# Attention's 128-row scores in a fused two-block kernel: three products of split operands in place of one f32 product

## The reference, cut to what matters

```python
q = (rms_norm(q_lat, q_norm) @ w_q_up).reshape(B, S, 16, 128 + 64)
kv = (rms_norm(kv_lat, kv_norm) @ w_kv_up).reshape(B, S, 16, 128 + 128)
q_nope, k_nope, v = q[..., :128], kv[..., :128], kv[..., 128:]
# q_rope, k_rope: the 64 rotary rows, k_rope shared by the heads
s = (einsum('bqhd,bkhd->bhqk', q_nope, k_nope)
     + einsum('bqhr,bkr->bhqk', q_rope, k_rope)) * ATTN_SCALE
p = softmax(where(causal, s, -1e30))          # in blocks of 128 queries
o = einsum('bhqk,bkhd->bqhd', p, v)
out = (o.reshape(B, S, 2048) * silu(z)) @ w_out
```

## Time and profile before

| what | us |
|---|---|
| median of three runs | 2210.17 |
| lowest and highest | 2209.99 and 2212.29 |
| the profiled execution's own time | 2210.97 |
| span of its trace | 2209.2 |
| TensorE busy (PE) | 2172.9, 98% |
| VectorE (DVE), ScalarE (ACT), GpSimd (POOL) busy | 1074.0, 939.5, 1068.4 |

### The profile page before, as it was taken

One profiled execution on the slowest core, in us unless ns is written; L12 is line 12 of the kernel. 1 busy time (PEld: TensorE's weight loads), 2 busy tenths in 40 slices (PEclk: granted clock), 3 DMA queues, 4 the chain that ended last, 5 costly groups with the idle time before them and its releaser, 6 DMA issues.

```text
span 2209.2 us, 33303 instructions
## 1 busy us (share of the span) xinstructions
PE 2172.9 (98%) x10972; PEld 1772.6 (80%) x10972; DVE 1074.0 (49%) x1498; ACT 939.5 (43%) x1638; POOL 1068.4 (48%) x787
## 2 busy tenths in 40 slices
PE   8999999999999999999999999999999999999999
PEld 6888888888888888788778878888778777888886
DVE  7842224444442262666524832236666638666512
ACT  4343333444433343555433244334454645444422
POOL 5654445445454444444355654444431634555553
PEclk9999999999999999999999999999999999999999
DMA  4332323233322333211132233333220022233333
GB/s 141 95 105 95 95 86 105 95 97 100 97 95 95 100 95 95 68 58 59 38 98 94 89 102 96 100 99 98 89 74 22 1 75 69 95 95 96 99 106 108
DMA packets 53791, 194.33 MB, mean 88 GB/s; under 512 B 6096, under 2 KB 6352, under 8 KB 53712
## 3 DMA queue, kind: packets, MB, share of 16 engines
q1 hardware_dynamic: 52704, 191.13, 27.5%
q10 hardware_dynamic: 1008, 2.14, 0.3%
HBM read 191.14 MB, written 2.10 MB: 87 GB/s over the span
## 4 chain that ended last, share of the span: by engine, by line
PE 73%; issue 15%; POOL 9%; DVE 1%; ACT 1%; POOLq 0%; DVEq 0%; ACTq 0%
PE proj L692 19%; PE proj L693 19%; PE proj L694 19%; POOL w_lo L621 9%; PE aux L850 2%; PE proj L875 1%; PE proj L803 1%; PE proj L805 1%; PE proj L804 1%; PE aux L861 1%; PE proj L973 1%; PE aux L973 1%; PE proj L1261 1%; PE proj L1262 1%; PE proj L1263 1%
## 5 line engine op out<-in xcount | busy, mean ns | idle before, releaser
L621 POOL TENSOR_TENSOR w_lo<-w_stage,w_hi 128x512 fp32r<-128x512 f32 x716 | 989.8, 1389 | 995.2 <-ACT w_hi L1323 995.0
L1323 ACT ACTIVATE w_hi<-w_stage 128x512 fp32r<-128x512 f32 x716 | 442.4, 628 | 805.3 <-PE proj L694 741.3
L692 PE MATMUL proj<-xh,w_hi 128*128 128x512 f32 x1696 | 666.3, 393 | 1.2 <-POOL w_lo L621 1.2
L694 PE MATMUL proj<-xh,w_lo 128*128 128x512 f32 x1696 | 660.1, 389 | 0.0
L693 PE MATMUL proj<-xl,w_hi 128*128 128x512 f32 x1696 | 660.1, 389 | 0.0
L692 PEld LDWEIGHTS proj<-xh,w_hi 128*128 128x128 f32 x1696 | 318.4, 188 | 74.6 <-POOL w_lo L621 5.6
L693 PEld LDWEIGHTS proj<-xl,w_hi 128*128 128x128 f32 x1696 | 318.4, 188 | 67.7 <-issue 2.4
L694 PEld LDWEIGHTS proj<-xh,w_lo 128*128 128x128 f32 x1696 | 318.4, 188 | 66.4
L692 PE MATMUL proj<-act_h,w_hi 128*128 128x512 f32 (+1 forms) x840 | 327.1, 389 | 2.8 <-POOL w_lo L621 2.8
L694 PE MATMUL proj<-act_h,w_lo 128*128 128x512 f32 (+1 forms) x840 | 326.8, 389 | 0.0
L693 PE MATMUL proj<-act_l,w_hi 128*128 128x512 f32 (+1 forms) x840 | 326.8, 389 | 0.0
(11 more groups left out here) (344 smaller groups left out, 2345.5 us busy)
## 6 DMA issues: line engine op xcount, KB each, us to landing
w_stage<-stream SPq DMA_DIRECT2D x358, 512.0 KB, 3.5
out<-x_res SPq DMA_DIRECT2D x3, 512.0 KB, 2.6
x_res<-x SPq DMA_DIRECT2D x2, 512.0 KB, 8.2
consts_sb<-consts ACTq DMA_DIRECT2D x1, 640.0 KB, 4.0
x_res<-x ACTq DMA_DIRECT2D x1, 512.0 KB, 7.5
out<-x_res SPq DMA_DIRECT2D x2, 256.0 KB, 2.2
x_res<-x SPq DMA_DIRECT2D x1, 256.0 KB, 3.5
x_res<-x ACTq DMA_DIRECT2D x1, 256.0 KB, 5.0
```

What stands on the lines that cost most here:

```text
L621: pool.tensor_tensor(w_lo[:, at, :], w_stage[:, at, :], w_hi[:, at, :].bitcast(F32), ALU.subtract).then_inc(stage_free, 1)
L692: pe.matmul(o, w_hi[:, slot, cols], hi, start=(b == 0), stop=False)
L694: mm = pe.matmul(o, w_lo[:, slot, cols], hi, start=False, stop=(b == blocks - 1))
L1323: act.activation(w_hi[:, u % RING, :], w_stage[:, u % RING, :], ACT.Copy).then_inc(hi_done, 1)
```

## The change

- The operands `qn` and `kn` (f32) are replaced by high and low parts in fp32r: `q_even` and `q_odd` for pairs of even and odd number, and `k_parts`, which is kept once and not twice. `qr` is kept once as well. Two placeholders move where tiles lie in SBUF.
- ScalarE now copies each q and k tile from its up-projection bank (`q_hi`, `k_hi`); VectorE waits for that (`q_high`, `k_high`) and subtracts the high part from the same bank; the bank is free after the subtraction.
- TensorE makes three fp32r products for each head and row block.
- ScalarE's list: q_hi(p+1, 0) comes after heads_hi(p-1) and before copy_turned(p, 0); q_hi(p+1, 1) after the w_hi that follows it; k_hi(0) after copy_turned(p, 2), then rope_hi(p+1), k_hi(1) and only then the w_hi that stood before rope_hi. In front of the loop q_hi twice, three w_hi, k_hi(0), rope_hi(0), k_hi(1), one w_hi.
- VectorE's and TensorE's lists keep their order; GpSimd and SyncE are not touched.

```diff
--- before.py
+++ after.py
@@ -350,15 +352,20 @@
...
-        qn = sb("qn", [P, 2, 2, S], F32, over)
-        kn = sb("kn", [P, 2, 2, S], F32, over)
-        qr = sb("qr", [P, 2, S], F32, over)
+        q_even = sb("q_even", [P, 2, 2, S], F32R, over)
+        k_parts = sb("k_parts", [P, 2, 2, S], F32R, over)
+        qr = sb("qr", [P, S], F32, over)
...
@@ -455,6 +462,7 @@
         k_rot_done = sem("k_rot_done")
         k_rope_hi, k_rope_lo = sem("k_rope_hi"), sem("k_rope_lo")
         q_rope_hi, q_rope_lo = sem("q_rope_hi"), sem("q_rope_lo")
+        q_high, k_high = sem("q_high"), sem("k_high")
         ready = sem("ready")
         dve_step = sem("dve_step")
         consts2_loaded = sem("consts2_loaded")
@@ -541,6 +549,11 @@
         def two_norms(n):
 
             return phases[n + 1] == "mixer"
+
+        HIGH, LOW = range(2)
+
+        def q_part(p, h, part):
+            return q_odd[2 * part + h][:, :] if p % 2 else q_even[:, part, h, :]
 
         def up_bank(j):
             return proj[:, 2 + j % 2, :]
@@ -847,7 +860,10 @@
                         pe.wait_ge(pt_done, n - 1)
                     q = slice(qb * P, w)
                     for h in range(2):
-                        pe.matmul(score_banks(qb, w)[:, h, :], qn[:, p % 2, h, q], kn[:, p % 2, h, 0:w], start=True, stop=False)
+                        o, q_h, q_l = score_banks(qb, w)[:, h, :], q_part(p, h, HIGH), q_part(p, h, LOW)
+                        pe.matmul(o, q_h[:, q], k_parts[:, HIGH, h, 0:w], start=True, stop=False)
+                        pe.matmul(o, q_h[:, q], k_parts[:, LOW, h, 0:w], start=False, stop=False)
+                        pe.matmul(o, q_l[:, q], k_parts[:, HIGH, h, 0:w], start=False, stop=False)
                     for h in range(2):
                         pe.matmul(score_banks(qb, w)[:, h, :], q_rope[:, h, q], k_rope_h[:, 0:w], start=False, stop=False)
                         mm = pe.matmul(score_banks(qb, w)[:, h, :], q_rope[:, h, q], k_rope_l[:, 0:w], start=False, stop=True)
@@ -1447,6 +1463,18 @@
                         act.activation(k_rope_h[:, :], k_rot[:, :], ACT.Copy).then_inc(k_rope_hi, 1)
                 assert unit.n == attention_unit + 4
                 v_tiles = iter([j for j, (kind, _, _) in enumerate(UP_TILES) if kind == "v"])
+                q_tiles = iter([j for j, (kind, _, _) in enumerate(UP_TILES) if kind in ("q0", "q1")])
+                k_tiles = iter([j for j, (kind, _, _) in enumerate(UP_TILES) if kind in ("k0", "k1")])
+
+                def q_hi(p, h):
+                    j = next(q_tiles)
+                    up_ready(act, j, attention_unit)
+                    act.activation(q_part(p, h, HIGH), up_bank(j), ACT.Copy).then_inc(q_high, 1)
+
+                def k_hi(h):
+                    j = next(k_tiles)
+                    up_ready(act, j, attention_unit)
+                    act.activation(k_parts[:, HIGH, h, :], up_bank(j), ACT.Copy).then_inc(k_high, 1)
 
                 def take_v(quad, blk):
                     j = next(v_tiles)
@@ -1475,15 +1503,20 @@
                     act.wait_ge(up_taken, 6 * p + 5)
                     for h in range(2):
                         half = slice(64 * h, 64 * h + 64)
-                        act.activation(q_rope[half, h, :], qr[half, p % 2, :], ACT.Copy).then_inc(q_rope_hi, 1)
+                        act.activation(q_rope[half, h, :], qr[half, :], ACT.Copy).then_inc(q_rope_hi, 1)
 
                 def heads_hi(p):
                     for h in range(2):
                         act.wait_ge(og_done, 2 * p + h + 1)
                         act.activation(act_h[:, 2 * p + h, :], og[:, h, :], ACT.Copy).then_inc(ah_done, 1)
 
-                his(4)
+                q_hi(0, 0)
+                q_hi(0, 1)
+                his(3)
+                k_hi(0)
                 rope_hi(0)
+                k_hi(1)
+                his(1)
                 for blk in range(4):
                     take_v(0, blk)
                 his(2)
@@ -1495,9 +1528,12 @@
                         his(1)
                     if p:
                         heads_hi(p - 1)
+                    if more:
+                        q_hi(p + 1, 0)
                     copy_turned(p, 0)
                     if more:
                         his(1)
+                        q_hi(p + 1, 1)
                     copy_turned(p, 1)
                     expo(p, 2)
                     if more:
@@ -1505,8 +1541,10 @@
                     expo(p, 3)
                     copy_turned(p, 2)
                     if more:
+                        k_hi(0)
+                        rope_hi(p + 1)
+                        k_hi(1)
                         his(1)
-                        rope_hi(p + 1)
                     copy_turned(p, 3)
                     if p < HEAD_PAIRS - 2:
                         take_v(p // 2 + 1, 2 * (p % 2))
@@ -2006,26 +2044,30 @@
                     return up_bank(j)
 
                 def take_q(p, h):
-                    took(dve.tensor_copy(qn[:, p % 2, h, :], next_up()))
+                    b = next_up()
+                    dve.wait_ge(q_high, 2 * p + h + 1)
+                    took(dve.tensor_tensor(q_part(p, h, LOW), b, q_part(p, h, HIGH).bitcast(F32), ALU.subtract))
 
                 def take_rope(p):
                     b = next_up()
                     link(dve.tensor_tensor(q_sin[:, :], b, sn[:, :], ALU.mult))
-                    took(dve.tensor_tensor(qr[:, p % 2, :], b, cs[:, :], ALU.mult))
+                    took(dve.tensor_tensor(qr[:, :], b, cs[:, :], ALU.mult))
 
                 def take_swap(p):
-                    took(dve.tensor_tensor(qr[:, p % 2, :], qr[:, p % 2, :], next_up(), ALU.add))
+                    took(dve.tensor_tensor(qr[:, :], qr[:, :], next_up(), ALU.add))
 
                 def rope_lo(p):
 
                     dve.wait_ge(q_rope_hi, 2 * p + 2)
                     for h in range(2):
                         mine, other = slice(64 * h, 64 * h + 64), slice(64 - 64 * h, 128 - 64 * h)
-                        dve.tensor_tensor(q_rope[other, h, :], qr[mine, p % 2, :], q_rope[mine, h, :].bitcast(F32),
+                        dve.tensor_tensor(q_rope[other, h, :], qr[mine, :], q_rope[mine, h, :].bitcast(F32),
                                           ALU.subtract).then_inc(q_rope_lo, 1)
 
                 def take_k(p, h):
-                    took(dve.tensor_copy(kn[:, p % 2, h, :], next_up()))
+                    b = next_up()
+                    dve.wait_ge(k_high, 2 * p + h + 1)
+                    took(dve.tensor_tensor(k_parts[:, LOW, h, :], b, k_parts[:, HIGH, h, :].bitcast(F32), ALU.subtract))
 
                 def row_max(p, qb):
```

More of the change, by code:

```diff
@@ L306, in program @@
         k_rope_l = sb("k_rope_l", [P, S], F32R, stat_over)
+        sb("sums_and_cosines", [P, 2, S], F32, stat_over)
+        q_odd = [sb("q_odd0", [P, S], F32R, stat_over)]
         stat_over.close()
@@ L352, in program @@
         lat_h = sb("lat_h", [P, 5, S], F32R, over)
-        k_rot = sb("k_rot", [P, S], F32, over)
+        turned_over = ExitStack()
+        k_rot = sb("k_rot", [P, S], F32, turned_over)
+        turned_over.close()
+        q_odd.append(sb("q_odd1", [P, S], F32R, over))
         zs = sb("zs", [P, IT, S], F32, over)
@@ L356, in program @@
         q_sin = sb("q_sin", [P, S], F32, over)
-        qn = sb("qn", [P, 2, 2, S], F32, over)
-        kn = sb("kn", [P, 2, 2, S], F32, over)
-        qr = sb("qr", [P, 2, S], F32, over)
+        q_even = sb("q_even", [P, 2, 2, S], F32R, over)
+        k_parts = sb("k_parts", [P, 2, 2, S], F32R, over)
+        qr = sb("qr", [P, S], F32, over)
+        q_odd.append(sb("q_odd2", [P, S], F32R, over))
         sn = sb("sn", [P, S], F32, over)
         og = sb("og", [P, 2, S], F32, over)
+        q_odd.append(sb("q_odd3", [P, S], F32R, over))
         over.close()
```

## The result

The changed kernel took 2228.81 us (median of four, 2227.76 to 2229.42) where the kernel before took 2211.23 on the same chip (2209.99 to 2212.31): **slower by 0.79%**, ratio 1.0079 with a 95% interval of 1.0067 to 1.0090. The profiled execution took 2227.76 us with a span of 2226.0, 16.8 longer than the span before. The forecast was +11.0 us, so the direction and the two stalls were right and the size was not: 2228.81 lies 1.8 us outside the range.

The account below looks back on a forecast made before the run. TensorE, 98% busy at full clock, was taken as the bound, with other engines deciding at two waits. Terms -5.2 + 12.2 + 3.0 + 0.7 + 0.3 = +11.0 us gave a median of 2221.2 us, range 2214.5 to 2227.

Parts of the forecast that it names:

- the two stalls: TensorE waits longer for k0's bank, 1.74 us in seven turns, and for ScalarE's turned copy, 0.5 us in six pairs.
- products: Attention scores: three fp32r products replace each f32 product, gaining 0.65 us per pair, 5.2 us for eight pairs.
- k banks, seven: k1 waits for ScalarE's copy and VectorE's subtraction of k0: 1.74 us later in seven turns, 12.2 us.
- q banks, six: q_hi(p+1, 0) ahead of copy_turned(p, 0) delays row block 2's scores 0.5 us in pairs 1 to 6: 3.0 us.
- start: In pair 0, k1 and v1 wait for ScalarE's copies of k, so the scores begin 0.7 us later.
- moved his(1): ScalarE's w_hi copy, moved behind k_hi(1), is used some 7 us later, so the delay costs nothing.
- last turn beside its k and products: Without v tiles, k1's load to the next scores takes 5.4 us instead of 5.1, for rope_lo: +0.3 us.
- an engine busy 43%: ScalarE's low average load, cited for banks free in time, at best 2205 us; that rival had 9%.
- GpSimd's scaling: GpSimd's 1.85 us scaling ends 2.1 us after k1 starts; TensorE turns that block at 2.9, covered by 0.8.
- covered by 1.2: Counted from k1's start, rope_lo ends at 5.4 us and the next pair's scores come at 6.6: no wait.
- Rival (c): Chain from swap to rope_lo outruns its 1.2 us cover, each instruction 0.2 to 0.3 us longer; about 2228 us; 9%.

Follow-up runs that it names:

- w_hi late: Changed kernel with ScalarE's his(1) moved from in front of copy_turned(p, 3) to behind it: 2223.14 us, ratio 1.0057.
- k by VectorE: Changed kernel with VectorE making both parts of k, a copy and then the subtraction out of the bank: 2217.36 us, ratio 1.0031.
- k's copy first: Changed kernel with ScalarE's k_hi(0) ahead of copy_turned(p, 2): 2223.63 us, ratio 1.0059.
- q behind: Changed kernel with ScalarE's q_hi(p+1, 0) moved behind copy_turned(p, 0): 2226.15 us, ratio 1.0066.
- three together: Changed kernel with his(1) behind copy_turned(p, 3), q_hi(p+1, 0) behind copy_turned(p, 0) and values(p, 2) ahead of k_up(1): 2221.86 us, ratio 1.0036.
- values between: Changed kernel with TensorE's values(p, 2) ahead of k_up(1): 2227.36 us, ratio 1.0078.
- the last combination: Changed kernel with k by VectorE, q_hi behind the turned copy, values(p, 2) ahead of k_up(1), w_hi behind copy_turned(p, 3): 2214.35 us, ratio 1.0017.
- outputs early: First four output blocks put ahead of scores(7, 0): on the changed kernel 2226.99 us, ratio 1.0072; on the kernel before 2213.27 us, ratio 1.0011.
- the first combination: Changed kernel with k by VectorE, q_hi behind the turned copy, w_hi ahead of rope_hi, first output blocks early: 2213.02 us, ratio 1.0012.
- the products alone: Kernel before with q and k rounded to fp32r and three fp32r products for each f32 one, low parts left out: 2207.87 us, ratio 0.9986.

## Why the prediction was right and where it was wrong

| term | predicted | measured |
|---|---|---|
| products | -5.2 | -4.4 (alone, stage time) |
| k banks, seven | +12.2 | +12.6 (1.80 each) |
| q banks, six | +3.0 | +2.9 (0.49 each, by taking it away) |
| start | +0.7 | +0.86 |
| moved his(1) | 0 | +3.8 (by taking it away; 1.5 of it the clock) |
| last turn beside its k and products | +0.3 | +0.4 without his(1) |

The measured rows add up to 16.2 of the stage's 16.5; for the last of them, the stand in the last turn is 1.29 before and 1.7 with w_hi late.

**Right.** That TensorE's two places of waiting would each grow by what ScalarE puts ahead of the bank's release, and by how much; that the products gain; that an engine busy 43% does not help at a place where it is busy; that GpSimd's scaling stays covered.

**The step that failed** is the sentence "The moved his(1) delays a w_hi that is used two products of the next pair on, some 7 us later: nothing", with the one that rests on it, "the scores come at 6.6 and find rope_lo done at 5.4, covered by 1.2". I asked only who waits for the moved copy. I did not ask what it sets off: w_hi releases GpSimd's w_lo, and its new place puts w_lo 0.12 us ahead of rope_lo. (Before, a w_lo ran from 940.95 to 942.22 and rope_lo began at 942.14, an overlap of 0.08 us that cost nothing.) VectorE is then held up until GpSimd is done, 1.72 us for an operation of 0.69, and the chain that had 1.2 us of cover has about none: scores of block 0 come 0.16 us later after k1 in an ordinary turn, and the last turn's stand is 1.0 longer. The Trainium skill, "SBUF — State Buffer", section Who interferes with whom, says that a VectorE instruction with two SBUF inputs contends with a GpSimd instruction that reads SBUF, that such contention is an exclusive lock on a shared pair of ports, and that the order of issue decides who blocks. The traces agree: VectorE takes 1.72 us beside a w_lo that started first, and w_lo takes 1.74 instead of 1.29 where VectorE started first (k by VectorE). Rival (c) had the right place, rope_lo outrunning its 1.2 us, at 9%, and a wrong cause: it was to come from each instruction running 0.2 to 0.3 us longer, and each ran as long as before but this one. Its price, up to 1 us a turn, was too high for the ordinary turns, where 0.22 was measured, and it had nothing for the clock; that its 2228 us is close to the measured 2228.8 is luck.

**The last turn** was priced by its wait alone. That TensorE's clock can drop behind a stand was in no term: 1.55 us of the change's time is TensorE doing the same products slower after it. The rows of before show no drop there, where it stood 1.29 us.

**The products** were sized 0.65 a pair and are 0.55 by the turn, 0.8 us too much gain in all: the rope rows gave the steps to within 0.09 us a block, at 384 keys the furthest.

Of the 7.6 us between 2221.2 and 2228.8, 5.8 lie between the spans (16.8 against 11.0). The rest is in how executions scatter: the profiled one of before stood 0.8 us over its median, that of after 1.05 under its own.

**Not settled.** What decides whether the clock drops: the changed kernel and the one with k's copy first stood 2.70 us each, one with a drop and one without. The start's 0.86 us was not tried by itself; with k by VectorE 0.75 of it is still there, so ScalarE's copy of k is not most of it. The 0.3 us between the terms and the stage is not placed.

## What to carry to other kernels

For each instruction that a change moves, follow what it releases and what that then runs beside. Here a VectorE subtraction with both inputs in SBUF lost about the rest of the GpSimd subtraction that had started before it, and the cover of a chain holds only if no such pair falls in it. The profile shows this as a longer busy time of the same instruction and not as a wait, so compare mean durations by form between two kernels. A bank whose release goes through two engines in sequence is bound to the first one's queue; if the second engine has time, let it do both (k by VectorE won 1.3 us of the 2.0 that a turn had lost). Work put into a gap of TensorE pays only if the chain behind the gap is not already what the next stage waits for, and if it does not uncover a wait where it came from; look at both before moving anything.

## What the hardware showed that I had not expected

- **VectorE and GpSimd.** Subtractions with both inputs in SBUF: 0.69 us alone; 1.72 (rope_lo, 64 rows by 512) and 1.81 (k_rope_l, 128 by 512) when GpSimd's subtraction began just before. GpSimd's subtraction, 1.29 us, took 1.74 when VectorE's had begun 0.11 us before. VectorE's subtraction of q's high part out of the PSUM bank (L2049 of the changed kernel), one input in SBUF, has a mean of 692 ns; seven of the sixteen start while a w_lo runs, and these take 0.69 us as well.
- **The clock after a stand.** Ahead of scores(7, 0), stands of 2.7 us (changed kernel, q behind), 2.8 (three together), 3.8 (values between), 1.8 (k by VectorE, windows of 0.56 and 0.59 behind) and 2.2 (the last combination, 0.51 and 0.64) were followed by a lower granted clock for some 3 to 7 us; 1.29 (before), 1.7 (w_hi late) and one of 2.7 (k's copy first) were not. The length of the stand does not tell which. With outputs early TensorE stands 1.9 us in all ahead of scores(7, 2), on either kernel with the drop behind it and in the first combination without. The stand of 2.24 us at the stage's end is the same in every trace; behind it the clock is 0.56 in the products alone and 1.00 in the kernel before. In the changed kernel the low clock cost about as much as the longer stand ahead of it: 1.6 us and 1.4.
- **fp32r products of 128 columns** have steps of 0.11 us, and those of 256 columns 0.12: the narrow ones are hardly cheaper. At 128 keys six of them took 0.62 us where four f32 records had taken 0.44; from 256 keys on the three products win.
